# Eight adaLN modulation blocks of layer 1 moved from the differential attention to between the turnings of the latent heads

## The reference

```python
m = jax.nn.silu(cond) @ ada_w + ada_b          # ada_w is 1024 x 6144
sh1, sc1, g1, sh2, sc2, g2 = jnp.split(m[:, None, :], 6, axis=-1)
h = rms_norm(x, n1_g) * (1.0 + sc1) + sh1
x = x + g1 * mixer(h)
h = rms_norm(x, n2_g) * (1.0 + sc2) + sh2
x = x + g2 * f(h)
```

## Time and profile before

| | |
|---|---|
| median of 3 runs | 1473.11 us (1472.83 to 1475.87) |
| profiled execution, its own time | 1476.61 us |
| its span | 1474.7 us |
| TensorE busy | 1316.5 us, 89% |
| VectorE busy | 919.4 us, 62% |
| ScalarE busy | 755.2 us, 51% |
| mean granted TensorE clock | 0.909 of full speed |

### The profile page before, as it was taken

How to read it: one execution, slowest core, us unless ns; L and a number is a source line. 1 busy time by engine, 2 the same in 40 slices (tenths; PEclk the granted TensorE clock), 3 DMA queues, 4 the chain that set the end, 5 groups by cost and what they waited for, 6 DMA issues and landing times.

```text
span 1474.7 us, 19664 instructions
## 1 busy us (share of the span) xinstructions
PE 1316.5 (89%) x7731; PEld 1142.1 (77%) x7731; DVE 919.4 (62%) x1199; ACT 755.2 (51%) x1076; POOL 225.5 (15%) x188
## 2 busy tenths in 40 slices
PE   4798998899999998886984898999999999999995
PEld 1695556799889986884663688889898898898894
DVE  0566686553434344665558543788688788788776
ACT  2445453543223325224444423677677777777773
POOL 0304670200020012000000011002203113113113
PEclk8698589999999998996995797899999999999998
DMA  9834676233444253321751003398899899899882
GB/s 323 212 121 143 200 229 200 86 115 115 128 143 129 94 163 130 115 72 44 262 160 59 1 2 117 122 338 297 282 319 301 280 331 313 286 328 312 285 280 95
DMA packets 178359, 277.66 MB, mean 188 GB/s; under 512 B 7120, under 2 KB 105192, under 8 KB 178264
## 3 DMA queue, kind: packets, MB, share of 16 engines
q1 hardware_dynamic: 176040, 269.87, 55.5%
q0 software_dynamic: 2224, 6.49, 1.5%
HBM read 274.02 MB, written 2.31 MB: 187 GB/s over the span
## 4 chain that ended last, share of the span: by engine, by line
PE 74%; DVE 14%; ACT 5%; issue 4%; DMA 2%; POOL 0%; DVEq 0%; SPq 0%; ACTq 0%
PE psB L1325 5%; PE psB L1327 5%; PE psB L1326 5%; PE psB L1775 4%; PE psB L1777 4%; PE psB L1776 4%; PE psA L1775 3%; PE psA L1777 3%; PE psA L1776 3%; PE psB L1406 3%; PE psA L1440 3%; DVE Wl L2360 3%; PE psA L1325 2%; PE psA L1326 2%; PE psA L1327 2%
## 5 line engine op out<-in xcount | busy, mean ns | idle before, releaser
L2360 DVE TENSOR_TENSOR Wl<-raw,Wh 128x1408 fp32r<-128x1408 f32 (+2 forms) x144 | 248.3, 1743 | 60.5 <-ACT Wh L1225 59.8
L1838 DVE TENSOR_TENSOR Wl<-raw,Wh 128x2048 fp32r<-128x2048 f32 (+4 forms) x64 | 133.9, 2097 | 143.0 <-ACT Wh L926 142.8
L1225 ACT CAST Wh<-raw 128x1408 fp32r<-128x1408 f32 (+2 forms) x144 | 197.8, 1375 | 32.5 <-PE psA L1777 16.5
L926 ACT CAST Wh<-raw 128x2048 fp32r<-128x2048 f32 (+4 forms) x64 | 110.0, 1724 | 136.2 <-PE psB L1549 64.2
L1775 PE MATMUL psA<-Wh,hTh 128*128 128x352 f32 x360 | 119.8, 333 | 0.7 <-ACT hTl L1231 0.7
L1777 PE MATMUL psA<-Wh,hTl 128*128 128x352 f32 x360 | 117.5, 326 | 0.0
L1776 PE MATMUL psA<-Wl,hTh 128*128 128x352 f32 x360 | 117.3, 326 | 0.0
L1325 PE MATMUL psB<-Wh,hTh 128*128 128x256 f32 (+2 forms) x332 | 100.4, 302 | 11.8 <-DVE kv L1946 4.7
L1326 PE MATMUL psB<-Wl,hTh 128*128 128x256 f32 (+2 forms) x332 | 99.2, 299 | 0.0
L1327 PE MATMUL psB<-Wh,hTl 128*128 128x256 f32 (+2 forms) x332 | 99.1, 299 | 0.0
L1406 PE MATMUL psB<-raw,cpad 128*32 128x256 f32 x768 | 68.1, 486 | 16.6 <-DMA raw<-in_l_ada_w 16.1
(11 more groups left out here) (347 smaller groups left out, 3459.0 us busy)
## 6 DMA issues: line engine op xcount, KB each, us to landing
raw<-in_l_moe_w SPq DMA_DIRECT2D x108, 704.0 KB, 5.6
raw<-in_l_ada_w SPq DMA_DIRECT2D x48, 1024.0 KB, 5.2
raw<-in_l_ffn_w SPq DMA_DIRECT2D x28, 1024.0 KB, 5.3
raw<-in_l_moe_w SPq DMA_DIRECT2D x27, 768.0 KB, 6.4
gate_b<-in_l_moe_w SPq DMA_DIRECT2D x18, 768.0 KB, 6.8
gate_b<-in_l_moe_w SPq DMA_DIRECT2D x18, 704.0 KB, 5.7
raw_tail<-in_l_moe_w SPq DMA_DIRECT2D x18, 704.0 KB, 4.9
raw<-in_l_w_in SPq DMA_DIRECT2D x11, 1024.0 KB, 5.3
```

Of the source, the lines that this page charges most:

```text
L926: act.copy(hi_of(u), raw_of(u)).then_inc(hi_ready, 1)
L1225: act.copy(half_of(Wh, h), raw_half(h)).then_inc(half_hi, 1)
L1838: dve.tensor_tensor(lo_of(u), raw_of(u), hi_of(u).bitcast(F32), ALU.subtract).then_inc(lo_ready, 1)
L2360: dve.tensor_tensor(half_of(Wl, h), raw_half(h), half_of(Wh, h).bitcast(F32), ALU.subtract).then_inc(half_lo, 1)
```

## The change

Of the 16 late blocks, eight (the two gates) stay in the differential attention, behind heads 8 to 15. The other eight (second shift and scale) go to the preparation of the latent heads: the first product ahead of the first turning, and behind the two turnings of each item one spread and one product; the last spread stands ahead of the latent attention. Their rows lie in `otok`. Loads follow: the eight blocks stand in SP's order behind the latent projections' units and ahead of the output weights. The limit of splitting is now the last latent unit for these projections, and the first two output weights are split in the latent attention, at head 8 on ScalarE and in iteration 9 on VectorE. Waits are set accordingly.

```diff
@@ -51,8 +51,9 @@
 NCG = P // CG
 FRONT, EARLY, LATE = ADA // 3, ADA, 2 * ADA // 3
 PREP_ASIDES = 2
-LATE_FROM = 6
+DIFF_BLOCKS, DIFF_FROM = 8, 8
 LAT_SPLIT = 23
+LAST_SPLIT = 8
 OUT_SPLIT = 23
 AHEAD = S - 1
 
@@ -297,11 +298,14 @@
 
 
 
+        late = FRONT + EARLY
         order = ([("block", d) for d in range(FRONT)] + [("unit", u) for u in range(base["out", 0])] +
-                 [("block", d) for d in range(FRONT, FRONT + EARLY)] +
+                 [("block", d) for d in range(FRONT, late)] +
                  [("unit", u) for u in range(base["out", 0], base["lat", 1])] +
-                 [("block", d) for d in range(FRONT + EARLY, FRONT + EARLY + LATE)] +
-                 [("unit", u) for u in range(base["lat", 1], n_units)])
+                 [("block", d) for d in range(late, late + DIFF_BLOCKS)] +
+                 [("unit", u) for u in range(base["lat", 1], base["out", 1])] +
+                 [("block", d) for d in range(late + DIFF_BLOCKS, late + LATE)] +
+                 [("unit", u) for u in range(base["out", 1], n_units)])
         place = {entry: n % RING for n, entry in enumerate(order)}
         landed, count = [], [0] * RING
         for u, (pieces, _, _) in enumerate(units):
@@ -488,7 +492,9 @@
 
             if u < base["out", 0]:
                 return base["out", 0] - 1
-            return base["lat", 1] - 1 if u < base["lat", 1] else n_units - 1
+            if u < base["lat", 1]:
+                return base["lat", 1] - 1
+            return base["out", 1] - 1 if u < base["out", 1] else n_units - 1
 
 
 
@@ -663,17 +669,20 @@
 
 
 
-        blocks = ([(0, u) for u in range(FRONT)] + [(0, u) for u in range(FRONT, ADA)] +
-                  [(1, u) for u in range(ADA)])
+
+
+        blocks = ([(0, u) for u in range(ADA)] + [(1, u) for u in range(3 * YC)] +
+                  [(1, u) for u in range(5 * YC, ADA)] + [(1, u) for u in range(3 * YC, 5 * YC)])
         EARLY_0, LATE_0 = FRONT, FRONT + EARLY
+        PREP_0, PREP_END = LATE_0 + DIFF_BLOCKS, LATE_0 + LATE
         ada_w = [rows(A[f"l{l}_ada_w"]) for l in range(2)]
 
         def aside_at(a, s):
 
             if a == 0 and PREP_ASIDES + s < EARLY:
                 return EARLY_0 + PREP_ASIDES + s
-            if a == 1 and LATE_FROM <= s < LATE_FROM + LATE:
-                return LATE_0 + s - LATE_FROM
+            if a == 1 and DIFF_FROM <= s < DIFF_FROM + DIFF_BLOCKS:
+                return LATE_0 + s - DIFF_FROM
             return None
 
         def aside_raw(d):
@@ -685,6 +694,8 @@
         def aside_rows(d):
             if d < FRONT:
                 return arow[:, d, :]
+            if d >= PREP_0:
+                return otok[:, d % 2 * YN:(d % 2 + 1) * YN]
             return work[:, 2016 + d % 2 * YN:2016 + (d % 2 + 1) * YN]
 
         def aside_bank(d):
@@ -1056,6 +1067,8 @@
                         split_to(ou)
                     if a == 1 and s == LAT_SPLIT:
                         split_to(base["lat", 1])
+                    if a == 2 and s == LAST_SPLIT:
+                        split_to(base["out", 1] + 1)
                     if a == 1 and s % 4 == 1 and s > 4:
                         square_root(stats[:, 12:14], stats[:, 10:12], 1.0 / P, eps_rms)
                         table_of(ACT.Exp)
@@ -1197,6 +1210,7 @@
             squares(2, 0)
             squares(2, 1)
             qk_root(QK, MLA_H)
+            aside_out(PREP_0)
             for m in range(NT + 4):
                 if m + 1 < NT + 4:
                     qk_root(QK, MLA_H, MLA_H * ((m + 1) % 2))
@@ -1206,6 +1220,9 @@
                 for half in range(2):
                     transposed_in(g0 + 2 * m + half,
                                   (qT2 if m < NT else kT2)[0:QK, 4 * half:4 * half + 4, t * P:(t + 1) * P])
+                spread_out(PREP_0 + m)
+                aside_out(PREP_0 + m + 1)
+            spread_out(PREP_END - 1)
             attend(2)
             for j in range(YC):
                 step(base["out", 1] + j)
@@ -1661,7 +1678,7 @@
                 last.then_inc(psT_full, 1)
             pe.wait_ge(psT_free, g0 + 7)
             attend(1)
-            pe.wait_ge(spread_free, LATE_0 + LATE)
+            pe.wait_ge(spread_free, PREP_0)
             pe.wait_ge(hT_lo, H["latT"] + 3)
             for j in range(2):
                 unit_b(base["lat", 1] + j, first["lat"]["B"] + NT * j, (hTh[:, 4:6, :], hTl[:, 4:6, :]))
@@ -1669,6 +1686,8 @@
             for j in range(2):
                 unit_b(base["lat", 1] + 2 + j, first["lat"]["B"] + 2 * NT + 4 * j, ck, 4)
             g0 = first["prep2"]["T"]
+            pe.wait_ge(psB_free, first["attend2"]["B"])
+            aside_product(PREP_0)
             for n in range(14):
                 pe.wait_ge(z_ready, Z2 + n // 2 + 1)
                 free_t(g0 + n)
@@ -1677,6 +1696,10 @@
                     src = qm[:, n // 2 % NT, h * QK:(h + 1) * QK]
                     last = pe.transpose(psT[(g0 + n) % 2][0:QK, j * P:(j + 1) * P], src, ident)
                 last.then_inc(psT_full, 1)
+                if n % 2:
+                    aside_spread(PREP_0 + n // 2)
+                    aside_product(PREP_0 + n // 2 + 1)
+            aside_spread(PREP_END - 1)
             pe.wait_ge(psT_free, g0 + 14)
             attend(2)
             out_projection()
@@ -1857,7 +1880,7 @@
 
             def mods(l, w):
 
-                dve.wait_ge(spread_free, (FRONT, FRONT + 3 * YC, LATE_0, LATE_0 + 3 * YC)[2 * l + w])
+                dve.wait_ge(spread_free, (FRONT, FRONT + 3 * YC, LATE_0, PREP_END)[2 * l + w])
                 at = V_ADA + (2 * l + w) * 2 * KD
                 both = mod[:, 2 * w:2 * w + 2, :, :].rearrange("p k f c -> p (k f) c")
                 link(dve.tensor_tensor(both, both, vecs[:, at:at + 2 * KD].unsqueeze(2).to_broadcast([P, 2 * KD, 2]),
@@ -2006,6 +2029,8 @@
                         split_to(ou)
                     if a == 1 and i == LAT_SPLIT + 1:
                         split_to(base["lat", 1])
+                    if a == 2 and i == LAST_SPLIT + 1:
+                        split_to(base["out", 1] + 1)
                     if i >= 2 and (i - 2) % per == per - 1:
                         rows_ready(a, (i - 2) // per)
                     if i >= 2:
```

## The result

The changed kernel took 1487.51 us (median of 14 runs, 1483.39 to 1496.53); the kernel before took 1478.73 us in the 14 runs beside it. The ratio is 1.006 with an interval of 1.0035 to 1.0086: slower, by 5 to 13 us. The forecast was 5 us slower. The profiled execution took 1487.37 us (span 1485.4, clock 0.906; before 1474.7 and 0.909). The ratios leave out three executions in the slow state (1675.53, 3115.08 and 4158.73 us, of experiments 6 and 7 and of the kernel before).

What follows compares the result with a forecast made beforehand. TensorE was taken to carry 74% of the chain of waits, VectorE 14%. Stage terms -1 - 8 + 8 + 6 = +5 us on the profiled 1476.61 gave 1481.6, as median 1478; range 1465 to 1488 with 8 in 10.

Steps and rivals of the forecast that it cites:

- rival B: Half clock in both the differential attention's last six heads and the preparation: +15 us, 1488; chance 12%.
- Differential attention, -1 forecast: Eight blocks fewer save 10.8 us of TensorE, mostly lost to waits and clock: -1 us, bounds -5 and +4.
- two gate waits: Differential attention: spreads wait for gate additions queued behind VectorE's row groups, twice, some 2 us each, as before.
- bare row group's 2.2 us: Differential attention, iteration 21: without a block's cover, VectorE's row group leaves TensorE standing 2.2 us.
- The clock term, 5.5 us: Differential attention at 1.2 GHz: 3.5 us for two of the last six heads, 2 us for heads at 692.
- the two terms of 1 us for waits: Differential attention: 1 us for the half-covered row group in iteration 9, 1 us for output transposes in iteration 20.
- Latent projections, -8 forecast: Two splits leave this stage, so TensorE no longer idles for banks: -8 us, or 7 if VectorE's copies don't keep up.
- Rival D: Latent projections gain only 4 us of 8 because something else holds the stage: +9 in sum, 1482; chance 8%.
- Preparation, +8 forecast: Eight blocks added between the turnings: +8 us, between +3 at 2.4 GHz and +11 at 1.2 GHz.
- Latent attention, +6 forecast: Two splits at head 8 delay the next minimum 4.8 us, plus 1.3 for clock: +6 us, bounds 4.5 and 8.
- The clock term, 1.3 us: Latent attention: behind the stands at the splits, one or two heads run at 1.2 GHz, +1.3 us.
- Rival A: Clock reaches 2.4 GHz in the preparation and stays, decided by mean clock over about 0.8: -5 us, 1468; chance 26%.

Runs made afterwards that it cites:

- experiment 6: Changed kernel with the two output-weight splits taken apart, casts behind heads 6 and 14, and their subtractions on GpSimd instead of VectorE: ratio 1.0031.
- 7: Changed kernel with gates behind every second head, ScalarE's root and squares ahead of its row copy, and splits apart on GpSimd: 1471.53 us, ratio 0.9937.
- experiment 10: The kernel combining every-second-head gates, root first and GpSimd splits, with seven blocks in the preparation and nine in the differential attention: 1466.64 us, ratio 0.9903.
- experiment 4: Changed kernel with its eight gate blocks behind every second head (8, 10, ... 22) instead of eight in a row: 1474.29 us, ratio 0.9964.
- experiment 1: Kernel before with only the new split limit, two output weights split in the latent attention, no block moved: 1479.91 us, ratio 0.9998.
- experiment 5: Changed kernel with ScalarE's copy of the product's rows placed behind the next root and squares in the preparation: 1487.1 us, ratio 1.005.
- experiment 9: Changed kernel with gates behind every second head and splits apart on GpSimd, keeping the old order on ScalarE in the preparation: 1473.94 us, ratio 0.9953.
- experiment 11: Same kernel as experiment 10, with ScalarE's two casts behind heads 2 and 6 of the latent attention instead of 6 and 14: 1467.69 us, ratio 0.9927.
- experiment 2: Changed kernel with the two output weights split among the latent projections again, so only the blocks move: 1489.27 us, ratio 1.0055.

## Why the prediction was right, and where it was off

The direction and size hold: forecast +5 us, stages +6.1, medians +8.8. The last two differ by 2.7 us, within the interval of the ratio; whether these stages cost more in most executions than in the profiled one, or something ahead of them does, the runs do not tell. As the kernel before itself came out 5.6 us higher than in the three runs shown first (median 1478.73 for 1473.11), 1487.51 is the upper edge of the range, next to rival B's 1488 and far above 1478; against the kernel before beside it the error is 4 us, and B's +15 is 6 too much.

**Differential attention, -1 forecast, +1.0 measured.** The two gate waits stayed, as said, at 2.04 us. The bare row group's 2.2 us did not appear: at half clock VectorE's 3.8 us of it fit beside heads of 3.7 us, and TensorE was never idle from 744 to 762. The clock term, 5.5 us, was the mis-sized one. I counted two heads of the last six at 1.2 GHz and a few ahead of 692; all the last ones were, and the clock came up only at 708. By the windows' clocks, the time at half clock is 52 us of the stage (0.30 x 2 x 87.34) where it was 24 before (0.14 x 2 x 86.32). That is rival B's condition for this stage, though its price of +4 is 3 us off and the -1 is 2. Without the 2.2, the forecast's terms are -10.8 + 1 + 1 = -8.8, and the measured +1.0 leaves 9.8 us for the clock. The busy times say the same more directly: 10.8 us of work went, busy time rose by 1.5 and idle time fell by 0.5, so some 12 us are slower work on what stayed, and the two terms of 1 us for waits do not show. Ten of the additional 28 us at half clock lie at the start, where the first product stands two heads later; experiment 10 puts it back. What the runs show is that the placing of the blocks decides it: experiment 4 took 12.2 us off, 10.9 of them in busy time on the same work.

**Latent projections, -8 forecast, -6.7 measured** (-7.8 in experiment 1). VectorE's eight copies follow each other without a gap, TensorE waits for no bank (in the kernel before 4.7 us), and the gain is within 0.3 us of the 7 that the forecast gave for copies that don't keep up. Rival D is refuted.

**Preparation, +8 forecast, +3.4 measured: the term that was most off.** It came out near the lower bound of 3. I chose the bound for 1.2 GHz because the first attention, full of products, runs at 0.50. The stage's clock rose from 0.55 to 0.77, with turnings at either level. The Trainium skill's rule, that activity releases the throttled clock (TensorE: Matmul & The Clock Gate, "What's actually happening"), which the forecast weighed and set aside, told the direction rightly here. It is no help in the last heads of the differential attention: there TensorE was busy 18.00 of 18 us at 0.50. The mechanisms named were right. ScalarE's queue behind the product costs 1.0 and 0.3 us in the second and fourth interval; experiment 5 takes exactly these away, and experiment 9 shows the order to be worth 2.75 us when the gates stand at every second head. The sixth interval costs 0.9: its turning is still at 1.94 us, and the next one follows with no wait, as TensorE's own work. The tail costs 1.2 us (5.63 for 4.47), but that compares a last turning at 2.4 GHz with one at 1.2. At like clocks it is 2.2 (6.63 in experiment 5 for 4.47), or 1.9 at the full one (5.63 for the 3.71 of experiment 11, which has no last product): a little less than the 2.4 of the lower bound, and at half clock far from the 4.4 of the upper.

**Latent attention, +6 forecast, +8.4 measured.** The wait at the ninth head is 4.7 us, as forecast (4.8). The clock term, 1.3 us, was too small: half until 848. By experiment 1 the splits alone cost 7.7 us, by experiment 2 the blocks alone 1.3, and experiment 6 takes 6.7 off.

So the sum was right partly by luck, because errors cancelled: +2.0, +1.3, -4.6 and +2.4. In each of the three larger ones the clock was taken at the wrong level for part of the stage. Rival A, a clock that comes up in the preparation and stays, had its first half: 0.77, just under the 0.8 from which it was to decide. The second half failed: the latent attention began at 0.50, behind a tail that ends with 1.56 us of waiting, and with one-key heads as before.

Of the signs that the forecast named, the two gate waits and the late minimum came as said. The latent squares began 1.9 us earlier (783.88 for 785.75), not 8 to 10; counted from the start of the first stage it is 5.7. From there to the first latent score it took 35.4 us at a clock of 0.77, just under the 36 to 43 and just over the 35 that would have made rival A right. The bare wait at the row group before the last did not come.

## What to carry to other kernels

When blocks of filler work leave a stage, price the clock as well as the time of the work: the eight blocks took 10.8 us of TensorE with them, and the stage became no shorter. Spread what stays evenly, here behind every second head, so that it neither queues behind a slow row group nor leaves a long stretch without it. And moving a split alone need not pay: the same two splits cost 7.8 us in one stage and 7.7 in the other. Apart and on GpSimd they cost 0.3 us (44.19 for 43.85) in one kernel and 5.6 (48.10 for 42.54) in another; which of the two, spacing or engine, did it was not tried.

## What the runs showed of the hardware

- A TensorE that by the profile never idles can stay at 1.2 GHz: 18.00 us busy of 18 at 0.50 in the last heads of the changed kernel. With products added between the same heads the clock rose during the second product at half clock (1.94, 1.61, then 1.07 us), and with the gate blocks at every second head it was 1.00 for 48 us with TensorE busy 41.28. What of the work decides it, the runs do not tell.
- The clock switches several times within one stage, and the switches move even where the code is the same: the sixth interval is 4.38 us in experiment 10 and 3.98 in 11, the differential attention 75.10 and 73.46, the preparation 36.23 and 35.01. Some stages repeat to 0.02 us over four kernels (87.33 to 87.35), but a stage time of a single profile can carry 1 to 2 us of this, and ratios near 1 need the medians.
- A row group of 3.8 us can cost nothing at 1.2 GHz: TensorE was busy 18.00 of 18 us beside one, with heads of 3.7 us. At 2.4 GHz the same heads show it: in experiment 4 the waits for the exponentials are 7.2 us for 3.5. So here the price of a stall and that of a low clock did not add.
